# A three-block attention network on one core: order of split-precision products in row panels, one GpSimd product per pair, and new slot tables

## The reference

```python
def first_block(x, ...):
    h = rms_norm(x, norm_gain)
    qa, ka, va, qb, kb, vb, ga, gb, mg = split(h @ w_in)
    ya = banded_attention(qa, ka, va, A_WINDOW, 1, bias, sink_a) * silu(ga)      # 8 heads
    outs, lses = dilated_group(...)                # 3 groups of 8 heads
    yb = sum(softmax(lses) * outs) * silu(gb)
    merged = sigmoid(mg + b)[0] * (ya @ w_branch_a) + sigmoid(mg + b)[1] * (yb @ w_branch_b)
    return x + merged @ w_out

def second_block(x, ...):
    for l in range(2):
        z = rmsnorm(x) @ w_in[l]
        o_nsa = gates * (compressed, selected and window attention of 8 heads)
        o_ret = retention(...)                     # 4 heads
        o_conv = conv_module(...)                  # 31 taps over 512 channels
        merged = sum_n(sigmoid(m_g[n]) * (branch_n @ w_branch[l, n]))
        x = x + merged @ w_out[l]
        x = x + square(relu(rmsnorm(x) @ w_ff1[l])) @ w_ff2[l]
    return rmsnorm(x)
```

## Time and profile before

| | |
|---|---|
| time, median of 3 runs | 1185.11 us |
| profiled execution, its own time | 1184.24 us |
| its span | 1182.4 us |
| TensorE busy (matmuls) | 1147.5 us, 97% |
| VectorE busy | 811.6 us, 69% |
| ScalarE busy | 591.0 us, 50% |
| GpSimd busy | 176.3 us, 15% |
| share of the chain that ended last: TensorE, DMA, GpSimd | 62%, 6%, 5% |

### The profile page before, as it was taken

The page is one execution under the profiler, slowest core; times in us unless marked ns, Lnnn a source line. Parts: engine busy times, 40 slices in busy tenths (PEclk is TensorE's granted clock), DMA queues, the critical chain, the costliest instruction groups (busy, mean ns, idle before and its releaser), DMA issues.

```text
span 1182.4 us, 16061 instructions
## 1 busy us (share of the span) xinstructions
PE 1147.5 (97%) x6223; PEld 953.0 (81%) x6223; DVE 811.6 (69%) x1252; ACT 591.0 (50%) x747; POOL 176.3 (15%) x201
## 2 busy tenths in 40 slices
PE   6999999999999999899999999999999999999997
PEld 5888777787998777787888888997777878888886
DVE  4666656656688789587777554698889587777453
ACT  5654575544435666443645433525575533655332
POOL 0232252200004235200000000004245100000000
PEclk9999999999999999999999999999999999999999
DMA  9656564457445667654555655545667554555550
GB/s 309 211 178 205 165 205 133 148 194 286 168 156 194 198 173 197 183 194 156 191 189 178 219 197 182 177 151 212 188 179 202 178 182 172 183 196 191 200 174 36
DMA packets 41628, 219.65 MB, mean 186 GB/s; under 512 B 4343, under 2 KB 14071, under 8 KB 16903
## 3 DMA queue, kind: packets, MB, share of 16 engines
q1 hardware_dynamic: 39392, 204.62, 50.0%
q0 software_dynamic: 1824, 13.78, 6.3%
q10 hardware_dynamic: 336, 0.22, 0.1%
HBM read 217.41 MB, written 1.20 MB: 185 GB/s over the span
## 4 chain that ended last, share of the span: by engine, by line
PE 62%; issue 15%; DMA 6%; DVE 6%; POOL 5%; ACT 4%; DVEq 2%; POOLq 0%; ACTq 0%
PE panel L938 15%; PE panel L940 14%; PE panel L939 14%; PE panel L984 5%; DMA ring_parts<-in_w_layers_dram 5%; PE tile L998 3%; POOL area L709 3%; PE panel L987 3%; DVE ring_parts L649 1%; PE panel L961 1%; PE panel L960 1%; PE panel L959 1%; ACT ring_parts L607 1%; DMA area_parts<-in_onehot_dram 1%; DVE area L2225 1%
## 5 line engine op out<-in xcount | busy, mean ns | idle before, releaser
L649 DVE TENSOR_TENSOR ring_parts<-ring,ring_parts 128x2048 fp32r<-128x2048 f32 (+1 forms) x173 | 389.9, 2259 | 156.5 <-ACT ring_parts L607 152.8
L607 ACT ACTIVATE ring_parts<-ring 128x2048 fp32r<-128x2048 f32 (+1 forms) x185 | 348.9, 1889 | 255.9 <-PE panel L940 203.3
L938 PE MATMUL panel<-ring_parts,hT 128*128 128x512 f32 (+2 forms) x688 | 277.2, 403 | 12.8 <-DMA ring_parts<-in_w_layers_dram 9.6
L940 PE MATMUL panel<-ring_parts,hT 128*128 128x512 f32 (+2 forms) x688 | 266.1, 387 | 0.0
L939 PE MATMUL panel<-ring_parts,hT 128*128 128x512 f32 (+2 forms) x688 | 265.8, 386 | 0.0
L938 PEld LDWEIGHTS panel<-ring_parts,hT 128*128 128x128 f32 x688 | 130.6, 190 | 50.2 <-issue 14.0
L940 PEld LDWEIGHTS panel<-ring_parts,hT 128*128 128x128 f32 x688 | 130.4, 189 | 27.0
L939 PEld LDWEIGHTS panel<-ring_parts,hT 128*128 128x128 f32 x688 | 130.6, 190 | 22.0
L938 PE MATMUL panel<-ring_parts,area_parts 128*128 128x512 f32 x376 | 147.2, 392 | 0.0
L939 PE MATMUL panel<-ring_parts,area_parts 128*128 128x512 f32 x376 | 146.9, 391 | 0.0
L940 PE MATMUL panel<-ring_parts,area_parts 128*128 128x512 f32 x360 | 140.6, 391 | 0.0
(11 more groups left out here) (250 smaller groups left out, 1248.4 us busy)
## 6 DMA issues: line engine op xcount, KB each, us to landing
ring<-in_w_layers_dram SPq DMA_DIRECT2D x140, 1024.0 KB, 4.9
ring<-in_w_first_dram SPq DMA_DIRECT2D x40, 1024.0 KB, 5.2
ring_parts<-in_w_layers_dram POOLq DMA_DIRECT2D x12, 1024.0 KB, 8.5
area<-bias_rows SPq DMA_DIRECT2D x16, 160.0 KB, 3.2
ring<-in_w_layers_dram SPq DMA_DIRECT2D x4, 560.0 KB, 3.9
area<-bias_rows SPq DMA_DIRECT2D x16, 96.0 KB, 3.0
area<-bias_rows SPq DMA_DIRECT2D x1, 1536.0 KB, 10.8
area<-in_gains_dram SPq DMA_DIRECT2D x3, 512.0 KB, 5.5
```

What stands on the lines that cost most here:

```text
L607: act.activation(ring_lo[:, SLOTS + hi, 0:w], ring[:, slot, 0:w], ACT.Copy).then_inc(high_ready, 1)
L649: g.tensor_tensor(ring_lo[:, slot, 0:w], ring[:, slot, 0:w], ring_lo[:, SLOTS + hi, 0:w], ALU.subtract).then_inc(low_ready, 1)
L938: pe.matmul(ps[:, b, 0:width], high, hi[:, k, :], start=first, stop=False)
L940: mm = pe.matmul(ps[:, b, 0:width], low, hi[:, k, :], start=False, stop=last)
```

## The change

It has four parts. In `rows_out` every half but qa/0 and the last one of the last panel first waits only for its high part (`high_ready`), runs its 16 products with the high weights, six per slot in the first two slots and four in the third, then waits for the low part and runs the eight products with the low weights, two in the third slot and six in the fourth. On GpSimd one tensor-by-tensor product scales a whole pair in place of `scale_units`, with the coefficient broadcast along the columns, and raises `scaled` by two; in the layers the coefficient is first laid out in three spans per unit by two tiny products in place of one. The slot tables, TAPS_AT, LOW_ADDED_AT, NORM_AT and RET_ROOT_AT have new values. The transposes of the rotated heads wait for both blocks before the first. The core of the diff:

```diff
-LOW_ADDED_AT = {("vr", 7): "mg0/1", ("mg0", 6): "mg1/1", ("mg1", 7): "mg2/1", ("mg2", 6): "mg3/1", ("mg3", 7): "mg4/1", ("mg4", 5): "mg5/1"}
+LOW_ADDED_AT = {("vr", 7): "mg0/1", ("mg0", 6): "mg1/1", ("mg1", 7): "mg2/1", ("mg2", 5): "mg3/1", ("mg4", 0): "mg4/1", ("mg4", 5): "mg5/1"}
-NORM_AT = {("mg2", 3): 0, ("mg2", 6): 1}
-RET_ROOT_AT, CONV_ROOT_AT = ("mg2", 2), ("mg5", 1)
+NORM_AT = {("mg2", 4): 0, ("mg3", 1): 1}
+RET_ROOT_AT, CONV_ROOT_AT = ("mg2", 1), ("mg5", 1)
-FIRST_S = ((0,), (4,), (6,), (12,), (15, 17), (23, 24), (29, 31), (37, 39))
-FIRST_E = (3, 7, 10, 12, 19, 27, 32, 41)
-FIRST_N = (4, 7, 10, 16, 23, 28, 34, 44)
-FIRST_T = ((5, 5), (10, 10), (14, 15), (20, 20), (26, 26), (31, 33), (39, 39), (46, 48))
-FIRST_V = (7, 14, 16, 22, 29, 39, 41, 49)
-FIRST_GATES, FIRST_HIGH = (7, 13, 33, 40), (22, 23, 41, 52)
-LAYER_S = (0, 4, 11, 18, 25, 27, 35, 45)
-LAYER_E = (2, 5, 15, 23, 28, 33, 43, 50)
-LAYER_T = (6, 14, 19, 26, 33, 41, 47, 54)
-LAYER_V = (7, 15, 22, 30, 38, 43, 50, 55)
-LAYER_SUM, LAYER_HIGH = (30, 57), (31, 61)
-LAYER_OTHER = dict(cmpHk=5, cmpFk=10, ro0=14, ro1=7, cmpHv=12, cmpFv=14, rot=17, cmp2=15, cmpS=18, cmpN=21, PcT=22, R0=19, R2=23, Or0=33, Or1=31, oR=50, cv=57, cz=62)
+FIRST_S = ((0,), (4,), (6,), (12,), (15, 17), (23, 24), (30, 32), (37, 40))
+FIRST_E = (2, 7, 10, 12, 19, 26, 32, 41)
+FIRST_N = (3, 9, 10, 16, 24, 31, 34, 45)
+FIRST_T = ((5, 5), (10, 10), (14, 15), (20, 21), (26, 26), (31, 34), (39, 39), (47, 48))
+FIRST_V = (7, 14, 16, 23, 27, 39, 41, 50)
+FIRST_GATES, FIRST_HIGH = (7, 12, 31, 41), (21, 25, 40, 53)
+LAYER_S = (1, 3, 10, 18, 23, 27, 36, 44)
+LAYER_E = (1, 5, 16, 23, 27, 32, 43, 50)
+LAYER_T = (6, 12, 19, 26, 31, 41, 47, 54)
+LAYER_V = (8, 15, 22, 29, 40, 43, 51, 55)
+LAYER_SUM, LAYER_HIGH = (29, 57), (30, 61)
+LAYER_OTHER = dict(cmpHk=5, cmpFk=8, ro0=11, ro1=6, cmpHv=12, cmpFv=14, rot=17, cmp2=17, cmpS=19, cmpN=21, PcT=23, R0=19, R2=21, Or0=33, Or1=30, oR=48, cv=58, cz=62)
...
+            L = one("L").rearrange("p (s b j) -> p s b j", s=4, b=2)
+            if p < 4:
+                pair = L[:, 2 * p % 4:2 * p % 4 + 2, :, 0:TOKENS]
+                g.tensor_tensor(pair, pair, c.rearrange("p b u -> p u b").unsqueeze(3).broadcast_to([P, 2, NB, TOKENS]), ALU.mult)\
+                 .then_inc(scaled, 2)
+            else:
+                unit = L[:, 2 * p % 4]
+                g.tensor_tensor(unit, unit, c[:, :, 0:1].broadcast_to([P, NB, 2 * TOKENS]), ALU.mult).then_inc(scaled, 1)
...
-            g.tensor_tensor(c, c, gt[:, :, :, p // 2, 1 + p % 2], ALU.mult).then_inc(pool_step, 1)
+            gate, spans = gt[:, :, :, p // 2, 1 + p % 2], coef_of_spans[:, p % 2]
+            g.tensor_tensor(spans[:, :, 0], c[:, 0], gate[:, 0], ALU.mult)
+            g.tensor_tensor(spans[:, :, 1:3], c[:, 1].unsqueeze(2).broadcast_to([P, 2, 2]), gate[:, 1].unsqueeze(2).broadcast_to([P, 2, 2]),
+                            ALU.mult).then_inc(pool_step, 1)
             g.wait_ge(pool_step, next(pool_steps))
-            scale_units(g, two("L").rearrange("p (s j) -> p s j", s=4), (2 * p, 2 * p + 1), (slice(0, P), slice(P, 3 * P)))
+            pair = two("L").rearrange("p (s j t) -> p s j t", s=4, t=P)[:, 2 * p % 4:2 * p % 4 + 2]
+            g.tensor_tensor(pair, pair, spans.unsqueeze(3).broadcast_to([P, 2, 3, P]), ALU.mult).then_inc(scaled, 2)
...
-                    hi, lo = (w[:, 0:4 * width].rearrange("p (k n) -> p k n", k=4) for w in wait_parts(part, half))
+                    if half == "qa/0":
+                        wait_parts(part, half)
+                    else:
+                        pe.wait_ge(high_ready, count(part, len(FIRST_HALVES), N_HALVES, index_of(part, half) + 1))
+                    hi, lo = (w[:, 0:4 * width].rearrange("p (k n) -> p k n", k=4) for w in parts_of(part, half))
+                    if half != "qa/0" and not (by_block and i == len(halves) - 1):
...
+                        for quarter in range(4):
+                            if quarter < 2:
+                                for n in range(3):
+                                    high_weights((3 * quarter + n) // 2, (3 * quarter + n) % 2)
+                            elif quarter == 2:
+                                for b in range(NB):
+                                    high_weights(3, b)
+                                wait_parts(part, half)
+                                for b in range(NB):
+                                    low_weights(0, b)
+                            else:
+                                for k in range(1, 4):
+                                    for b in range(NB):
+                                        mm = low_weights(k, b)
+                                mm.then_inc(done if i == len(halves) - 1 else half_used, 1)
+                            if plan:
+                                for e in plan[name, 4 * i + quarter]:
+                                    step(*e)
...
                         for b in range(NB):
-                            pe.wait_ge(rot_ready, l * 2 + (b + 1))
+                            pe.wait_ge(rot_ready, l * 2 + 2)
```

More of the change, by code:

```diff
@@ L702, in outputs_of_first @@
             return x[:, i // 2, 512 * (i % 2):512 * (i % 2 + 1)]
-        def scale_units(g, L, units_of, spans):
-            for u in units_of:
-                for b, at in enumerate(spans):
-                    e = g.tensor_scalar(L[:, u % 4, at], L[:, u % 4, at], coef[:, b, u:u + 1], None, ALU.mult)
-                e.then_inc(scaled, 1)
         pool_steps = itertools.count(1)
```

18 lines of the change are left out of this document (14 added, 4 removed).

## The result

The changed kernel took 1163.57 us (median of 4 runs, 1163.19 to 1164.1), where the kernel before took 1184.82 us beside it (4 runs, 1184.08 to 1185.86). The ratio is 0.9833, with a 95% interval of 0.9805 to 0.986. The change is worth 20 to 21 us, where 13.4 us were forecast: the direction was right and the sum too small.

The account below looks back on a forecast made before the run. TensorE, busy 1147.5 of 1182.4 us, was taken as the bound, through idle time and slow-clock stretches. 9.6 + 3.2 + 2.7 - 1.1 - 1.0 = 13.4 us off the 1185.11 us median gave 1171.7 us; range 1165 to 1180 us.

Parts of the forecast that it names:

- The transfer and the clock (9.6 + 3.2): TensorE's six waits for low weights by accumulating DMA go, 9.6 us; clock loss behind two of them goes, 3.2 us.
- Retention scores (2.7): Score product L1282 stops waiting for ScalarE's eviction, because cmpS moves behind it: gain 2.7 us over two layers.
- GpSimd's product (-1.1): One product per pair costs 3.1 or 4.1 us; the first block's pair 0 transposes wait longer: loss 1.1 us.
- New waits (-1.0): Tighter steps in the new tables and the joint wait for rotated blocks cost 1.0 us, bounds 0 and 5.
- likeliest case: The forecast itself, chance 0.66, own range 1167 us (no new waits, GpSimd waits gone) to 1175 us (new waits 4.3 us).
- One instruction would be stretched likewise: Beside VectorE's taps, GpSimd's single product would lengthen 1.74 times, as four products did: 3.8 to 7.1 us.
- VectorE's cover: VectorE's 8.86 us wait for TensorE's transposes after its taps shrinks to about 5 us, still waiting before its convolution statistics.
- The first (upper price): Rival: GpSimd's product costs its upper bound, giving 7.7 us back, 1179.4 us; chance 0.12.
- The second (a transfer stays): Rival: mg4/1's transfer still stops TensorE in each layer, perhaps with clock loss: 3 to 8 us back, 1175–1180 us; chance 0.09.
- The third (wider spacing): Rival: the new order widens matmul spacing; 4.3 ns each uses up the gain, 7 ns gives near 1194 us; chance 0.08.
- The fourth (TensorE merely arrives early and waits elsewhere): Rival: TensorE waits for ScalarE or VectorE in the same panels instead, clock falls as before, gain 0.6 us; chance 0.05.

Follow-up runs that it names:

- order alone: Kernel before with only the new order of products in `rows_out`; old GpSimd products, tables and waits for the rotated blocks: 1170.5 us, ratio 0.9903.
- tables alone: Kernel before with only the new slot tables and constants and the joint wait for the rotated blocks: 1176.32 us, ratio 0.9939.
- tables undone: Kernel after with all the old tables: 1168.66 us, ratio 0.9886.
- later transfer: Kernel after with the accumulating DMA of mg4/1 behind GpSimd's scaling of pair 7 instead of pair 6: 1179.53 us, ratio 0.9957.
- wait ahead: Kernel after, keeping the new matmul order, but TensorE waits for the low part before each half's first matmul: 1172.51 us, ratio 0.9916.
- first half: Kernel after with qa/0 also in the new order, each high and low piece awaited where first used: 1164.1 us, ratio 0.9821.
- GpSimd's product alone: Kernel before with only GpSimd's single tensor-by-tensor product per pair; order and tables as before: 1171.44 us, ratio 0.9915.
- order undone: Kernel after with the old `rows_out`: 1172.38 us, ratio 0.9921.

## Why the prediction was right in sign and short in size

**What bounds the kernel** was read rightly: TensorE's idle time and its slow stretches were where the time lay, and the whole gain came from there. The 20.1 us between the two spans are 9.6 (transfer) + 2.7 (retention scores) + 2.2 (transposes behind GpSimd) + 0.8 (first block, ScalarE) - 0.2 (new wait) = 15.1 us of idle time and 5.0 us of busy time, all behind the first 41 us.

**The transfer and the clock (9.6 + 3.2).** Right. The order alone gave 12.7 us against 12.8. Of the 5.0 us of busy time, 3.2 are the two stretches worked out beforehand; the other 1.8 us are not located, and the sum had no term for them. That a stop is followed by slow matmuls was read rightly for these two stretches, and is no rule: see the section on the hardware.

**Retention scores (2.7).** Right, and shown from both sides: gone with the tables alone, back with the tables undone.

**GpSimd's product (-1.1) is the term that failed**: it brought +2.2 us, a difference of 3.3. The step was the price. Both bounds were made from tensor-by-scalar products, in the belief that a second input could only cost more. It cost less, 1.47 and 1.90 us for the 3.1 and 4.1 taken, so that the transposes of the first pairs wait less and not more. Where no row shows a form of instruction, a bound from another form holds on neither side, and the prediction left no place below its lower bound.

**New waits (-1.0)** came to -0.2, and +0.8 had been overlooked: the old tables also made the first block wait for ScalarE, which is seen in the waits of before and had not been taken into the sum. Together a difference of 1.6 us.

So 13.4 + 3.3 + 1.6 + 1.8 = 20.1 us. By its ratio, 0.9833 x 1185.11 = 1165.3 us, the kernel lies at the lower end of the range; its own median, 1163.57 us, lies 1.4 us below it. The likeliest case's own range, from 1167 us, left out the time by either. Its lower end stood for a gain of 18.1 us and had the waits for GpSimd gone and no new ones; the 2.0 us beyond are the 0.8 of the first block and the 1.8 not located, less 0.4 of wait for GpSimd that stayed and the 0.2 of new wait. That the full range holds one of the two figures is in part luck: it had been stretched to 1165 us for stops too short to be listed, and not for a price with the wrong sign.

**"One instruction would be stretched likewise"** was wrong in its mechanism. The 1.74 times of four scalar products at 459.84 is no stretch. This is VectorE in the kernel before at that time:

```profile
461.38 2.33 DVE L649 TENSOR_TENSOR ring_parts<-ring,ring_parts 128x2048 fp32r<-128x2048 f32 x1
```

5.19 - 2.99 = 2.20 us is the time that this subtraction ran, from 461.38 to about 463.6: GpSimd stood still for one instruction of VectorE. The section on the hardware has the rest.

**VectorE's cover** was predicted at about 5 us and is nearly nothing. In the kernel after, VectorE's queue before the convolution statistics:

```profile
477.01 1.67 DVE L2267 SCALAR_TENSOR_TENSOR area<-area,cw 128x256 f32<-128x256 f32 x4
478.80 2.29 DVE L650 TENSOR_TENSOR ring_parts<-ring,ring_parts 128x2048 fp32r<-128x2048 f32 x1
481.01 1.29 DVE L2481 BATCH_NORM_STATS2 cns<-tile 128x6 f32<-128x512 f32 x2
```

```profile
471.31 0.82 PE L1040 MATMUL tile<-ident,area 128*128 128x128 f32 x6
```

There is no idle time in front of the statistics, where it was 8.86 us. The second fence is TensorE at the transposes of pair 7: 471.31 for 482.81, 11.5 us earlier, not the 5 us of the sum. VectorE's taps end only 481.77 - 478.68 = 3.1 us earlier, and a low part has moved into the gap. The cover held, but without reserve, and that sign was wrong.

**The rivals.** The first (upper price) fell: 1.47 us for its 4.1. Its own sum is also 1.0 us short: 1.3 + 3.8 + 2 x 1 + 1.6 = 8.7 us, not 7.7, which gives 1180.4 us, just above the stated range. The second (a transfer stays) fell: mg4/1 has 6.0 us of slack and the tightest transfer 0.8, though the experiment with the later transfer shows that its mechanism, its place and its clock loss are as described. The third (wider spacing) fell with the wait ahead. The fourth (TensorE merely arrives early and waits elsewhere) fell with the order alone: no new wait took the place of the old ones. It is what happened, however, with the first half, and VectorE would have been such a wait with the other two parts and the old order.

## What to carry to other kernels

Where a product is made of several and one operand is ready later than the others, put the products with the late operand last and wait for it there: that costs nothing and gives the late operand, here, 16 x 0.227 = 3.63 us, besides letting the tables of other engines fill their queues more freely. Before adding up the parts of a change, ask which of them remove the same wait: here three parts that were worth 31 us alone gave 20 together, and undone one by one they were worth 8.8, 5.1 and 3.1 us. An instruction form that no row shows should be priced with a bound on each side that comes from something else than a related form.

## What the runs showed of the hardware

**GpSimd and VectorE took turns for whole instructions.** The kernel with GpSimd's product alone, first GpSimd, then VectorE in order of time:

```profile
458.59 3.49 POOL L744 TENSOR_TENSOR area<-area,stat 128x768 f32<-128x768 f32 x1
```

```profile
458.45 2.29 DVE L650 TENSOR_TENSOR ring_parts<-ring,ring_parts 128x2048 fp32r<-128x2048 f32 x1
```

VectorE's subtraction starts first and keeps its usual 2.29 us. GpSimd's product starts 0.14 us later and ends at 462.08, 1.34 us after VectorE: about its own 1.47 us. The other way round, in the kernel after:

```profile
369.67 1.47 POOL L744 TENSOR_TENSOR area<-area,stat 128x768 f32<-128x768 f32 x1
```

```profile
369.77 1.40 DVE L2338 TENSOR_SCALAR stat<-stat 128x2 f32<-128x2 f32 x1
```

GpSimd is first and keeps 1.47 us; an instruction of VectorE with two columns, 0.17 us elsewhere, lasts until GpSimd is done. The Trainium skill says this in SBUF — State Buffer, section "SBUF: two separate sides": the two engines share a pair of ports as an exclusive lock, on VectorE's side for instructions with two inputs from SBUF or in a two-port mode, and whichever instruction starts first holds it to its end. The traces agree, with the numbers above.

VectorE's 12.6 us of additional busy time lie in few of its lines: 3.6 us in the 32 instructions of two columns (6.4 to 10.0 us), 3.2 in the taps (mean 485 to 498 ns), 2.2 in the low parts of whole halves, 2.0 in a normalisation of the retention outputs, 1.7 in two-column instructions of the first block. Number and kind of GpSimd's products both count: VectorE is busy for 824.2 us with one tensor-by-tensor product, 818.2 with four, 818.2 with one tensor-by-scalar product in the layers, and 812.7 with four. Four short ones can let VectorE in between. But the length of one instruction does not explain the rest, since the single scalar product takes 2.23 us and costs VectorE 6.0 us less than the single one of 1.47 us, where 813 us had been expected; why stays open.

**On GpSimd the product with two tensors was the faster one**, 1.47 us for 768 columns, with the coefficient read as a second tensor that repeats one value, against 2.23 us with a scalar per partition. Why was not tried.

**The clock fell behind some stops and not behind others, and their length did not tell which.** It fell behind those of 3.29 and 1.84 us in the kernel before, 3.52 us with the tables alone, 5.44 and 5.74 us with the later transfer, and, with GpSimd's product alone, behind two short ones of 1.32 and 0.43 us within 2 us. It stayed at 1.00 behind 3.10 us with the tables alone, 1.93 us with GpSimd's product alone, 1.86 us with the order undone and 1.62 us in the kernel before. Where it fell, the loss was 1.6 to 2.6 us. What decides was not tried; a stop that is taken away is worth its idle time for certain, and the clock's part only where the trace shows the slow matmuls behind it.
